# A decoder step in fp32 on one core: the last norm's reciprocal root on turned sums, and four small moves

## The reference

```
h = RMSNorm(x);  q,k,v,B,C,u,ga,gb = split(h @ w_in)
a = window attention(rope(q), rope(k), v);   b = B * dwconv3(C * u)
x = x + RMSNorm((sigmoid(ga)*(a @ w_a) + sigmoid(gb)*(b @ w_b)) @ w_o)
f = (gelu(dwconv3(RMSNorm(x) @ w_up_a) + bias) * (RMSNorm(x) @ w_up_g)) @ w_ffn_down
x = x + RMSNorm(f)                       # the "last norm" of this text
x = x + sigmoid(x @ w_ple_gate) * (p @ w_ple)
```

## Time and profile before

| | us |
|---|---|
| median of 3 runs | 2653.61 (2653.44 to 2654.08) |
| time of the profiled execution | 2653.8 |
| its span | 2652.0 |
| PE busy | 2642.8 |
| DVE busy | 2223.5 |
| ACT busy | 1386.6 |

### The profile page before, as it was taken

How to read it: one execution, slowest core, us unless ns; L and a number is a source line. 1 busy time by engine, 2 the same in 40 slices (tenths; PEclk the granted TensorE clock), 3 DMA queues, 4 the chain that set the end, 5 groups by cost and what they waited for, 6 DMA issues and landing times.

```text
span 2652.0 us, 55404 instructions
## 1 busy us (share of the span) xinstructions
PE 2642.8 (100%) x20929; PEld 2582.7 (97%) x20929; DVE 2223.5 (84%) x3908; ACT 1386.6 (52%) x2530; POOL 190.0 (7%) x289
## 2 busy tenths in 40 slices
PE   9999999999999999999999999999999999999999
PEld 8999999999999999999999999999999999999899
DVE  7988888888896687898888888888888768789987
ACT  6544545555563255655555555555555454445354
POOL 0221000000010000000000000000000000000000
PEclk9999999999999999999999999999999999999999
DMA  6676434333474455655566655665569575565674
GB/s 229 187 209 183 136 114 142 132 128 118 158 256 159 133 165 156 250 171 164 170 202 187 187 154 167 190 206 169 157 195 309 152 249 165 161 204 170 238 263 152
DMA packets 159884, 479.59 MB, mean 181 GB/s; under 512 B 17161, under 2 KB 51217, under 8 KB 156336
## 3 DMA queue, kind: packets, MB, share of 16 engines
q1 hardware_dynamic: 128608, 370.74, 39.8%
q0 software_dynamic: 30960, 106.59, 18.2%
q10 hardware_dynamic: 144, 0.15, 0.0%
HBM read 420.56 MB, written 55.71 MB: 180 GB/s over the span
## 4 chain that ended last, share of the span: by engine, by line
PE 96%; DVE 2%; issue 1%; ACT 1%; DMA 0%; SPq 0%; DVEq 0%; ACTq 0%
PE pair L1190 78%; PE pair L1155 6%; PE pair L1293 3%; PE pair L1271 3%; PE pair L1093 2%; PE pair L925 1%; PE pair L1250 1%; PE pair L1115 1%; PE pair L977 1%; PE pair L998 1%; DVE v_lo L1917 0%; DVE lo L2266 0%; PE pair L987 0%; PE pair L1058 0%; DMA s_raw<-in_sstream 0%
## 5 line engine op out<-in xcount | busy, mean ns | idle before, releaser
L1190 PE MATMUL pair<-o_hi,v_hi 128*128 128x260 f32 x5832 | 1653.9, 284 | 1.0 <-DVE v_lo L1917 0.5
L1190 PE MATMUL pair<-o_hi,v_lo 128*128 128x260 f32 x5832 | 1646.7, 282 | 0.0
L1358 ACT ACTIVATE v_hi<-s_raw 128x512 fp32r<-128x512 f32 (+1 forms) x1366 | 850.9, 626 | 937.1 <-PE pair L1190 793.1
L1190 PE MATMUL pair<-lo,v_hi 128*128 128x260 f32 x4164 | 1176.2, 282 | 0.0
L1917 DVE TENSOR_TENSOR v_lo<-s_raw,v_hi 128x512 fp32r<-128x512 f32 (+1 forms) x1286 | 872.8, 681 | 302.8 <-ACT v_hi L1358 265.9
L1190 PEld LDWEIGHTS pair<-o_hi,v_hi 128*128 128x128 f32 x5832 | 1096.5, 188 | 14.3 <-issue 12.1
L1190 PEld LDWEIGHTS pair<-o_hi,v_lo 128*128 128x128 f32 x5832 | 1098.3, 188 | 0.0
L1190 PEld LDWEIGHTS pair<-lo,v_hi 128*128 128x128 f32 x4164 | 782.6, 188 | 0.2
L1190 PE MATMUL pair<-lo_E,v_hi 128*128 128x260 f32 x834 | 236.0, 283 | 0.0
L1190 PE MATMUL pair<-lo_A,v_hi 128*128 128x260 f32 x834 | 235.2, 282 | 0.0
L1358 ACT ACTIVATE v_hi<-s_one 128x512 fp32r<-128x512 f32 (+1 forms) x220 | 137.0, 626 | 186.9 <-PE pair L1190 152.4
(11 more groups left out here) (273 smaller groups left out, 2498.1 us busy)
## 6 DMA issues: line engine op xcount, KB each, us to landing
s_raw<-in_sstream SPq DMA_DIRECT2D x468, 512.0 KB, 5.0
s_one<-in_sstream POOLq DMA_DIRECT2D x168, 512.0 KB, 5.4
raw<-f_scr SPq DMA_DIRECT2D x12, 1040.0 KB, 7.5
s_raw<-in_sstream SPq DMA_DIRECT2D x32, 384.0 KB, 4.1
g_scr<-d_h SPq DMA_DIRECT2D x16, 520.0 KB, 2.7
g_in<-g_scr SPq DMA_DIRECT2D x32, 260.0 KB, 2.8
x_scr<-y_sb SPq DMA_DIRECT2D x8, 1040.0 KB, 4.8
s_one<-in_sstream POOLq DMA_DIRECT2D x16, 384.0 KB, 4.9
```

The lines of the kernel that those rows point to most:

```text
L1190: mm = pe.matmul(out, wt[:, slot, kk * P:kk * P + P], r[:, k, :], start=j in (0, 1, 3) and k == 0 and n == 0, stop=k == nk - 1 and n == 2, ...
L1358: nc.scalar.activation(v_hi[:, n % 4, 0:width], src, ACT.Copy, scale=0.5 if halved(u) else 1.0).then_inc(v_hi_rdy, 1)
```

## The change

1. **Last norm.** The sums over partitions are turned: six small matmuls (`token_sums`) use spans of 87 tokens of the squares as stationary operand and one column of ones as moving operand, so that the sum of each token lands on a partition of its own, three columns for each half. ACT takes the root of 87 x 3 values for each half, DVE inverts these into `inv`. `spread` multiplies the broadcast column of `inv` with a unit matrix `spread_id`, three matmuls of 87 columns for each half, which puts the reciprocal roots of all tokens on all partitions in PSUM, and DVE's products read them there. `spread_id` is loaded by SP from `ident_in` (64 KB); it lies on `fs_s`, and is issued when the up projection's results are all out (`f_ready`), after the loads of the last down set in the program. PE waits for it ahead of `spread(1)`. The nine filling matmuls become three. Row 0 is handled by halves: `last_x` adds its second half first, and the plain unit takes that half first.
2. **Second down set.** The seventh product (j = 6) of its first unit is split, with its activations' parts made earlier on ACT and DVE, and DVE's low part of product 3 behind it.
3. **Fourth weight sum** of unit 1 in set 0 (`s4`): both halves move ahead of `o_low(2)`; `evac(u, 9)` moves up one place.
4. **A copy**: the last block of unit 31 (`LAST`, c21) is copied out of PSUM by ACT instead of by DVE.
5. **A table load** for the square root moves on ACT from the first conv unit to the third step of the branch products (`m == 2`).
6. Two semaphores of the rope become one, and PE's waits in the plain units are merged.

```diff
+        inv = at("inv", [P, 8], o[0])
+        spread_id = at("spread_id", [P, P], o[0] + 64)
...
         def in_fp32(u, j):
+            if set_of(u) == 4:
+                return is_first(u) and j < 6
...
         # SP, behind the last down set's loads
             for c in range(4):
                 sp.wait_ge(ple_stored[c], 16)
+            sp.wait_ge(f_ready, KF)
+            sp.dma_start(spread_id[:, :], ident_in).then_inc(tab_ready, 16)
             gate_in(0)
...
+            def token_sums(h, squares, first, last):
+                for b, t in enumerate(SPANS):
+                    mm = pe.matmul(pair[2][0:SPAN, h, 504 + b:505 + b], squares[:, t:t + SPAN], ones[:, 0:1],
+                                   start=first and b == 0, stop=last, skip_group_check=True)
+                if last:
+                    mm.then_inc(half_rdy, 1)
+            def spread(h):
+                pe.wait_ge(inverted, 2 - h)
+                for b, t in enumerate(SPANS):
+                    mm = pe.matmul(pair[2][:, h, t:t + SPAN],
+                                   inv[0:SPAN, 3 * h + b:3 * h + b + 1].to_broadcast([SPAN, P]),
+                                   spread_id[0:SPAN, 0:SPAN], start=True, stop=True, skip_group_check=True)
+                mm.then_inc(half_rdy, 1)
...
                 if s == S_GATE:
-                    half_sums(1)
-                    last_square(1)
-                    for n in range(9):
-                        pe.matmul(pair[3][:, n % 2, 0:HALF], ones[:, :], chan[:, 0:HALF],
-                                  start=True, stop=True)
+                    pe.wait_ge(sq_h_added, added_squares(1, 31))
+                    token_sums(1, sq_acc[:, 1, :], True, True)
+                    token_sums(0, sq_acc[:, 0, :], True, False)
+                    for n in range(2):
+                        pe.matmul(pair[3][:, 1, 0:HALF], ones[:, :], chan[:, 0:HALF], start=True, stop=True)
+                    pe.wait_ge(tab_ready, 16 * 8)
+                    spread(1)
+                    pe.wait_ge(sq_h_rdy, 64)
+                    token_sums(0, sq_h[:, 1, :], False, True)
+                    pe.matmul(pair[3][:, 1, 0:HALF], ones[:, :], chan[:, 0:HALF], start=True, stop=True)
+                    spread(0)
...
         # ACT
+                act.wait_ge(half_rdy, 5 - 2 * h)
+                nc.scalar.activation(inv[0:SPAN, 3 * h:3 * h + 3], pair[2][0:SPAN, h, 504:507], ACT.Sqrt,
+                                     scale=1.0 / D, bias=eps[0:SPAN, :]).then_inc(root_rdy, 1)
...
                 if u == LAST and i == 13:
+                    fourth(u, d[:, 1, 0:HALF])
                     cf_high(4)
...
-                    if u == U_BR and j == 5:
-                        warm(ACT.Sqrt, 2)
...
                 v_high(BR_S + 2 * m + 5)
+                if m == 2:
+                    warm(ACT.Sqrt, 2)
...
         # DVE, in last_x
+                token_invert(1)
+                dve.wait_ge(half_rdy, 4)
+                st.done(half_product(0, 1))
+                token_invert(0)
...
+                half_add(1)
+                st.done(half_product(1, 1))
+                dve.wait_ge(half_rdy, 6)
+                half_product(0, 0).then_inc(xu_rdy, 1)
+                half_product(1, 0).then_inc(xu_rdy, 1)
+                dve.wait_ge(xu_rdy, KD + 1)
+                half_add(0)
+                product(2)
...
+                add(1)
```

More of the change, by code:

```diff
@@ L2323, in early_unit @@
                 both_halves(s4, u)
+                if s == 4:
+                    o_low(s, 6)
+                    v_low(nxt - 2)
+                    v_low(nxt - 1)
+                    evac(u, 9)
+                    o_low(s, 3)
+                    both_halves(s3, u + 1)
+                    v_low(nxt)
+                    v_low(nxt + 1)
+                    evac(u, 11)
+                    both_halves(s2, u + 1)
+                    v_low(nxt + 2)
+                    v_low(nxt + 3)
+                    evac(u, 13)
+                    return
                 o_low(s, 3)
@@ L2376, in second_unit @@
                 for i in range(14):
-                    if i < 13:
+                    if i < 13 and not (s == 0 and i == 9):
                         evac(u, i)
+                    if s == 0 and i == 8:
+                        evac(u, 9)
+                    if s == 0 and i == 5:
+                        both_halves(s4, u)
                     if i in (0, 1) and s != 2:
@@ L2390, in second_unit @@
                         s1(u + 1, i - 2)
-                    if i in (6, 7):
+                    if i in (6, 7) and s:
                         s4(u, i - 6)
@@ L2608, in h_evac @@
                     cf_low({7: 0, 10: 1, 11: 2, 12: 3}[i])
-                if i == 13 and not 0 < u < U_CONV + 2:
+                if i == 13 and not 0 < u < U_CONV + 2 and u != LAST:
                     produced(u, 6)
@@ L2729, in new_x, with last_x, token_invert, gain @@
                         after[k]()
+                add(KD - 1)
+            def last_x():
+                def token_invert(h):
+                    dve.wait_ge(root_rdy, 6 - h)
+                    dve.reciprocal(inv[0:SPAN, 3 * h:3 * h + 3], inv[0:SPAN, 3 * h:3 * h + 3])\
+                       .then_inc(inverted, 1)
+                def gain(k):
+                    return chan[:, C_FFNPOST + k:C_FFNPOST + k + 1]
+                def half_product(k, h):
+                    row = y_sb[:, k, h * HALF:(h + 1) * HALF]
+                    return dve.scalar_tensor_tensor(out=row, in0=row, scalar=gain(k),
+                                                    in1=pair[2][:, h, 0:HALF], op0=ALU.mult, op1=ALU.mult)
+                def half_add(h):
+                    row = y_sb[:, 0, h * HALF:(h + 1) * HALF]
+                    dve.tensor_tensor(row, row, x_tile(0)[:, h, :], ALU.add).then_inc(xn_rdy, 1)
+                def product(k):
+                    dve.scalar_tensor_tensor(out=two(y_sb[:, k, :]), in0=two(y_sb[:, k, :]), scalar=gain(k),
+                                             in1=both(2), op0=ALU.mult, op1=ALU.mult).then_inc(xu_rdy, 1)
+                def add(k):
+                    if k % KH == 0:
+                        for t in (2 * (k // KH), 2 * (k // KH) + 1):
+                            dve.wait_ge(op_in[t], 96)
+                    dve.wait_ge(xu_rdy, KD + k + 1)
+                    dve.tensor_tensor(two(y_sb[:, k, :]), two(y_sb[:, k, :]), x_tile(k), ALU.add)\
+                       .then_inc(xn_rdy, 1)
+                token_invert(1)
+                dve.wait_ge(half_rdy, 4)
+                st.done(half_product(0, 1))
+                token_invert(0)
+                for t in range(2):
+                    dve.wait_ge(op_in[t], 96)
+                st.wait()
+                half_add(1)
[6 more added lines that the diff above has]
+                product(2)
+                st.wait()
+                add(1)
+                for k in range(3, KD):
+                    product(k)
+                    add(k - 1)
                 add(KD - 1)
```

87 lines of the change are left out of this document (53 added, 34 removed).

## The result

The changed kernel takes **2663.6 us** (median of 7 runs, 2662.9 to 2664.6); the kernel before takes 2654.0 beside it (7 runs, 2653.4 to 2654.4). The ratio is 1.0037, with a 95% interval of 1.0028 to 1.0047: 9.6 us or 0.37% slower. The forecast was 2662.0, within 2659.0 to 2665.5.

A forecast was written before the change was run, and what follows sets the result against it. PE was taken as the bound, busy 2642.8 of 2652.0 us. Norm +9.7, second down set -0.6, set 0 0, copy and table load -0.7 gave +8.4 on 2653.8; less 0.2 for the median, 2662.0 us, range 2659.0 to 2665.5 (82%).

The forecast's parts named there:

- The transfer: Last norm: spread_id lands at 2478.5 behind four quarters, PE waits 8.9 us; +7.9 us at full clock.
- rival (a): Last norm: spread_id lands in time, some 2 us after its issue; not slower, 2651.4 us; 10%.
- The serial part behind the landing: Last norm: spreads, sum, root, reciprocal and both rows follow the landing in full; row 1 through PE 7.15 us after it.
- The clock: Last norm: PE's idle wait drops it to 1.2 GHz until it has worked for a while; 1.8 us more taken.
- the norm's +9.7: Last norm in all: +7.9 us for the late transfer plus 1.8 for half clock, ends +7.9 and +10.5.
- Rival (b): Last norm: PE waits, but the clock stays up or returns at once; +6.6 us, 2660.2; 20%.
- (c): Last norm: half clock into row 2 or 3, or landing at 2479.5; 2663.5 to 2666 us; 15%.
- The norm without the transfer: Last norm with spread_id already there: shorter reciprocals against added spreads and halves, a gain of 0.9 us.
- The second down set: Its first unit: one fp32 product becomes split, -0.6 us, ends -0.6 and -0.2.
- rival (d): Second down set: DVE's lag costs more than the split product gains; +0.5 us on any case; 10%.
- Set 0: Set 0's weight sum: DVE's work only reordered, PE waits at 83.5 instead; 0 us, ends -0.2 and +0.2.
- Copy and table load: Conv units' end: copy to ACT brings 0.1 to 0.2, table load's 0.5 hole goes; together -0.7 us.

The follow-up runs named there:

- e1_early: The changed kernel with spread_id issued on SP's queue at the start of the third group of down units, not behind the four quarters: 2651.1 us.
- e7_reorder: The changed kernel with spread_id issued early and PE's order turned (one filler, sum of half 0, then spread(1) and spread(0)): 2651.0 us.
- e12_changed_again: The changed kernel itself, unedited, run again on the chip of the run with 24 fillers: 2664.2 us.
- e9_fill_behind: e7_reorder with two more fillers behind spread(0): 2650.8 us, ratio 0.9989 to the kernel before.

## Why the prediction was right, and where its sizes were off

**The transfer** was the step that decided. That `spread_id` cannot land before the four quarters ahead of it was right; `ident` at the start was the right witness, and rival (a) is out. The size was off: forecast for 2478.5 with PE where it was before; PE was 1.9 us earlier (the ledger's first four lines but for rounding), and it landed at 2477.6, so 1.0 us later against PE. The term took 10.1 us from the issue, as if that were a property of the transfer. It is the time at which the queue is through: issue to landing was 11.0, 10.0, 11.0, 9.8 and 9.5 us in five kernels with it in this place, but the landing was 118.2 to 118.4 us behind the first mark in all of them (the wait at 2368 taken off). Even so, the last quarter lands at 116.7 to 117.1 us behind that mark in the three kernels with the old norm, and at 117.9 to 118.6 in all eleven executions with the new one, also where nothing stands behind it but `pl_first`. The bytes moved by then are the same within some per cent. What differs is one packet of 16 KB that the trace lists under "instruction". In the changed kernel, at 2470 to 2471, and in the kernel before, at 2477 to 2478 (packets, MB, share of the 16 engines in this 1 us):

```profile
q8 instruction: 1, 0.02, 6.5%
...
q8 instruction: 1, 0.02, 6.4%
```

That is 1.03 to 1.06 us of one engine's time. It starts 109.6 to 113.8 us behind the first mark in all eleven, ahead of the quarters' landings, and at 116.3 or so, when the last quarter has all but landed, in the three with the old norm. Its time is about the difference. So it is the likely straggler, for which the prediction allowed 1 us; no run moved this packet alone, and why it comes earlier with the new norm stays open.

**The serial part behind the landing** at full clock: 7.15 - 3.54 = 3.6 us from the landing to the plain unit's start in effect. Measured where the clock stayed: 56.31 us from the first spread to the second mark (40 fillers), against 52.82 from the plain unit's start before, which is 3.5. Right.

**The clock**: the mechanism was right, the size too small. Taken were 1.8 us, ends 0 and 2.6; measured 2.7, by the two kernels side by side. The step that failed is "the clock may come back within row 0": it came back at 2485.8, when row 0 was through, 8.1 us after PE's first matmul. With +1.0 for the landing and +0.9 for the clock the norm's +9.7 becomes the measured +11.6. Rival (b) is out. What came is nearer to (c), which had 15%, than to the forecast: the measured 2663.6 lies in its range of 2663.5 to 2666. Of its two conditions the late landing held (2477.6 and the 1.9 us by which PE was early make 2479.5); the other did not, since the clock was back with the end of row 0, before row 2 or 3. The two errors went the same way, and the range was wide enough for both. Rival (a) gave the transfer some 2 us if the order of the queue didn't bind it; on a queue of its own it took 4.8, so even then PE would have waited and the clock fallen (2657.5 us).

**The norm without the transfer**: forecast -0.9, measured -1.2 (e1_early).

**The second down set**: -0.64 measured, -0.62 by the formula. DVE had 0.1 us of room by the working, and PE has no wait there; rival (d) is out. **Set 0**: PE's waits moved as said; one of 0.36 at 75.9 went, and one of 0.59 stands at 83.7 now, for DVE's low part:

```profile
83.74 0.36 PE L1204 MATMUL pair<-o_hi,v_hi 128*128 128x260 f32 x1 [0.42 <-DVE v_lo L1972]
```

The sum is zero, since DVE's work was only put in another order. **Copy and table load**: -0.94 against -0.7. The copy brings 0.34 instead of 0.1 to 0.2. Its price, the longer wait at 741.4, was right at 0.3; what was undervalued is that both waits behind DVE go, the one of 0.43 and the 0.10 that follows it.

The total came 1.6 above the forecast. 1.2 are the terms above (+1.9 for the norm, -0.45 for a wait that comes and goes, -0.2 for the conv units, +0.1 for the start), and 0.4 is that the kernel before measured 2654.0 in the later runs instead of 2653.6.

## What to carry to other kernels

A small load that something waits for was here as late as what stood ahead of it in its queue; its own size told nothing. Look for the first moment at which its place is free and issue it there: here one transfer moved turned +9.6 us into -2.6. A queue of its own helped less: at the same late moment it still left +3.8 us. And a place in which PE does only small matmuls for a few microseconds can be worth a filler in its gaps, up to its end: two of them kept the clock up here in all eleven executions. It pays where the work behind is PE's own and not already waiting for another engine.

## What the hardware showed that was not expected

- The clock can fall without a long idle time of PE. With small matmuls and gaps of 0.9 us at most it fell at 2470.3 (e7_reorder), and with gaps of 0.6 us at most at 2469.4 (without fillers), 3.5 to 4 us behind the last product of the down units, and stayed down for 3.4 us each time. Two fillers more, and it didn't.
- The fall may come after the idle time is over: 2.7 us after PE was back from 2.2 idle us (20 fillers), 0.6 us after it was back from 3.5 (ACT's queue). Where PE stood idle for about 10 us the clock fell 4.3 us into it in one execution of the changed kernel and 1.8 us into it in the other, e12_changed_again, whose stretches are below (2.7 us into it with the transfer behind two quarters):

```profile
2469.00:2473.00 4.00, 0.00 (x0) 0.00 (x0) 0.00 (x0) 0.00 (x0) 0.00 (x0) 0.69 1.08 392
2473.00:2474.00 1.00, 0.00 (x0) 0.00 (x0) 0.00 (x0) 0.00 (x0) 0.00 (x0) 0.50 0.98 385
```

- The half clock lasted 13.7 and 17.1 us in these two, 6.8 us with the wait of 3.5 us, 3.4 us in the three kernels with short gaps. Its price is not in proportion to that time: 2.7 to 3.1 us for the 13.7 and 17.1, of which 5.6 and 8.2 passed before the landing, and 0.6 to 1.0 us for 3.4 us (without fillers, and e7_reorder against e9_fill_behind).
- SP's issue of one 512 KB quarter took 0.7 to 2.1 us, in the same place of nearly the same kernels, and the landing did not move with it (the first quarter landed 9.3 to 9.8 us behind the start of its issue in all eleven with the new norm).
